# Output stages of a two-layer encoder step: gate rows requested ahead of the residual, weights split in place

## The reference

```
for layer in 0, 1:
    h = rms_norm(x, norm_g[layer]) * (1 + scale) + shift      # scale, shift, gate from the conditioning
    z = h @ w_in                                              # layer 0: 8 groups of 512 columns, and 2 index groups
    ...                                                       # attention of the layer, 16 heads of 64 columns
    mixed = attention_out * silu(gates_from_z)                # gates_nat in DRAM
    y = mixed @ w_out                                         # 1024 x 1024
    x = x + gate[:, None] * y
x = rms_norm(x, final_norm_g)
```

## Time and profile before

| | us |
|---|---|
| median of 3 runs | 2069.78 |
| the three runs | 2056.97, 2069.78, 2070.72 |
| the profiled execution's own time | 2069.88 |
| its span | 2068.1 |

### The profile page before, as it was taken

The page is one execution under the profiler, slowest core; times in us unless marked ns, Lnnn a source line. Parts: engine busy times, 40 slices in busy tenths (PEclk is TensorE's granted clock), DMA queues, the critical chain, the costliest instruction groups (busy, mean ns, idle before and its releaser), DMA issues. The chain is left out here.

```text
span 2068.1 us, 34383 instructions
## 1 busy us (share of the span) xinstructions
PE 1728.9 (84%) x12754; PEld 1335.7 (65%) x12754; DVE 1305.5 (63%) x2848; ACT 943.7 (46%) x1885; POOL 240.5 (12%) x337
## 2 busy tenths in 40 slices
PE   5693488999998985899996895979996999998697
PEld 2460256888876863677774674858774776776476
DVE  2632464787999953778886443661556777777554
ACT  4311252224611273668883213528654667776211
POOL 5000100000000102111100000000004222220000
PEclk8795686999999996999998997989997999999899
DMA  7465602442224318977754343342425111110532
GB/s 277 156 192 147 109 9 73 101 128 87 77 66 112 97 46 203 231 211 203 205 134 153 135 160 131 94 108 71 104 62 115 27 39 30 33 26 9 193 97 97
DMA packets 237102, 235.18 MB, mean 114 GB/s; under 512 B 148181, under 2 KB 172021, under 8 KB 234890
## 3 DMA queue, kind: packets, MB, share of 16 engines
q1 hardware_dynamic: 226170, 198.91, 35.5%
q0 software_dynamic: 10768, 34.08, 4.3%
HBM read 173.98 MB, written 58.95 MB: 113 GB/s over the span
## 5 line engine op out<-in xcount | busy, mean ns | idle before, releaser
L351 PE MATMUL PS<-ab_wh,hT 128*128 128x512 f32 x576 | 229.1, 398 | 10.4 <-DVE ab_wl L676 9.8
L353 PE MATMUL PS<-ab_wh,hT 128*128 128x512 f32 x576 | 225.4, 391 | 0.0
L352 PE MATMUL PS<-ab_wl,hT 128*128 128x512 f32 x576 | 225.0, 391 | 0.0
L1125 DVE TENSOR_SCALAR_CACHE_REDUCE topk_junk<-scores,topk_small 128x528 bf16<-128x528 f32 (+6 forms) x224 | 194.6, 916 | 1.3
L2205 DVE CUSTOM_DVE_ANT_0 la_S<-PS,la_mask 128x128 f32<-128x128 f32 (+3 forms) x144 | 107.6, 747 | 41.7 <-PE PS L353 28.5
L351 PE MATMUL PS<-out_wh,out_mT 128*128 128x512 f32 x288 | 121.9, 423 | 10.1 <-DVE out_wl L1693 9.7
L351 PEld LDWEIGHTS PS<-ab_wh,hT 128*128 128x128 f32 x576 | 108.7, 189 | 33.4 <-ACT ab_wh L604 6.7
L1471 ACT ACTIVATE at_P<-at_S,at_nm 128x128 f32<-128x128 f32 (+2 forms) x144 | 110.4, 767 | 31.3 <-DVE at_nm L1516 31.1
L353 PEld LDWEIGHTS PS<-ab_wh,hT 128*128 128x128 f32 x576 | 108.5, 188 | 23.3
L352 PEld LDWEIGHTS PS<-ab_wl,hT 128*128 128x128 f32 x576 | 108.9, 189 | 21.5
L352 PE MATMUL PS<-out_wl,out_mT 128*128 128x512 f32 x288 | 118.4, 411 | 0.0
(11 more groups left out here) (415 smaller groups left out, 4597.6 us busy)
## 6 DMA issues: line engine op xcount, KB each, us to landing
ab_w<-in_ab_w_in SPq DMA_DIRECT2D x64, 256.0 KB, 2.9
out_g<-scratch_gates_nat SPq DMA_DIRECT2D x18, 512.0 KB, 5.9
mod_ada_w<-in_ada_w SPq DMA_DIRECT2D x8, 1024.0 KB, 13.0
mod_w<-in_ada_w SPq DMA_DIRECT2D x16, 512.0 KB, 4.9
mod_w<-in_ada_w SPq DMA_DIRECT2D x8, 1024.0 KB, 5.8
at_kc<-in_cache_a_k SPq DMA_DIRECT2D x8, 1024.0 KB, 9.5
at_vc<-in_cache_a_v SPq DMA_DIRECT2D x8, 1024.0 KB, 8.0
at_kc<-in_cache_b_k SPq DMA_DIRECT2D x8, 1024.0 KB, 7.6
```

The costliest lines, as they stand in the source:

```text
L351: nc.tensor.matmul(out, x[0], w[0], start=start, stop=False)
L352: nc.tensor.matmul(out, x[0], w[1], start=False, stop=False)
L353: return nc.tensor.matmul(out, x[1], w[0], start=False, stop=stop)
L1125: go(V.tensor_scalar(mark, x, limit, 0.0, op, ALU.add, accum_out=cnt[:, m:m + 1]), 0 if m == M - 1 else 1)
```

## The change

- `mixed_out`: SP requests gate rows two tiles ahead: `load_x(i)`, then `load_gates(i + 2)`. The DVE has a written order: splits of weights between the first gate steps and low halves; then per tile y, the low half of tile i+2, the norm, and `gate_rows(i + 3)`. The last tile's y, square, scale and store go in two halves of 512 columns. TensorE turns tile 1 between the sixth and seventh k-tile of tile 0, and walks both column halves of tile 0 k by k.
- All weights have their own place: the raw tile and its low half share memory (`overlaid`), so `wl = raw - wh` is written over `raw`, and there is no ring. In `projection` all k-tiles of group g+1 are requested at step (g, 1), once the group before in that slot is multiplied, and split in steps 2 to 8.
- `OutLoads`: two k-tiles and the first gate rows of the output stage are requested inside the attention, in memory that the attention has done with (`decay`, `stage`, `qr_in` now lie there).
- `Front`: the first group's eight k-tiles of layer 1's projection and its norm rows are requested in stage 1 (behind x 2), and split there by ACT and DVE, two per tile in tiles 2 to 5. The block that loaded the norm rows is gone.
- `scores` lies at the other side of SBUF.

Core of the diff:

```diff
+def overlaid(nc, stack, name, shape, side="left"):
+    with nc.sbuf_tensor(f"{name}_raw", shape, F32, side=side) as raw:
+        pass
+    return raw, stack.enter_context(nc.sbuf_tensor(name, shape, F32R, side=side))
...
+    def fetch_weights(self, sp):                      # Front
+        c = self.c
+        sp.dma_start(c.latent_g[:, 0:QL], dram(c.i["c_q_norm_g"], 0, [[0, P], [1, QL]])).then_inc(self.g_in, 16)
+        sp.dma_start(c.latent_g[:, QL:], dram(c.i["c_kv_norm_g"], 0, [[0, P], [1, KVL]])).then_inc(self.g_in, 16)
+        for k in range(KT):
+            sp.dma_start(self.raw[:, k, :], c.i["c_w_in"][0, k * P:(k + 1) * P, 0:QL + KVL]).then_inc(self.w_in[k], 16)
+    def split_high(self, act, k):
+        act.wait_ge(self.w_in[k], 16)
+        self.nc.scalar.activation(self.wh[:, k, :], self.raw[:, k, :], ACT.Copy).then_inc(self.w_hi, 1)
+    def split_low(self, dve, k):
+        dve.wait_ge(self.w_hi, k + 1)
+        self.nc.vector.tensor_tensor(self.wl[:, k, :], self.raw[:, k, :], self.wh[:, k, :], ALU.subtract).then_inc(self.w_lo, 1)
...
-        split_steps.setdefault((g - 1, k * NT // groups[g].kt), []).append(k)
+            split_steps.setdefault((g - 1, 2 + k * (NT - 2) // groups[g].kt), []).append(k)
...
-            if r >= RING:
-                sp.wait_ge(w_lo, r - RING + 1)
+            if g:
+                sp.wait_ge(w_lo, first[g])
+            if before_in_slot(g) is not None:
+                sp.wait_ge(mm_done, NT * (before_in_slot(g) + 1))
+            for k in range(groups[g].kt):
+                for at, frm, m in parts:
+                    sp.dma_start(raw[slot(g)][:, k, at:at + m], groups[g].w[k * P:(k + 1) * P, frm:frm + m]).then_inc(w_in[k], 16)
...
+                if s < len(steps) and steps[s][1] == 1:
+                    load_weights(sp, steps[s][0] + 1)
...
+            sp.wait_ge(maxed, head_at(H - 1, QT - 1) + 1)     # end of branches_ab's SP list
+            out.fetch_weights(sp)
+            sp.wait_ge(built, 6)
+            out.fetch_gates(sp)
...
+            for k in range(2, KT):                            # mixed_out, SP
+                sp.dma_start(raw(k), out.w_dram[k * P:(k + 1) * P, :]).then_inc(w_in[k], 16)
+                if k == 3:
+                    load_gates(1)
+            load_x(0)
             sp.dma_start(gate[:], ...).then_inc(rows_in, 16)
-            sp.wait_ge(w_lo, KT)
+            sp.dma_start(sample_gate[:], ...).then_inc(rows_in, 16)
...
+            load_gates(2)
+            load_x(1)
+            load_gates(3)
             for i in range(2, NT):
-                rows(i)
+                load_x(i)
+                load_gates(i + 2)
+                if front and i == 2:
+                    front.fetch_weights(sp)
...
+            chain(nc.vector.reciprocal(rinv[:], c.sums[:]))   # mixed_out, DVE
+            gate_rows(0)
+            for k in range(2):
+                split_low(k)
+            low(0)
+            for k in range(2, 4):
+                split_low(k)
+            gate_rows(1)
+            for k in range(4, KT):
+                split_low(k)
+            low(1)
+            gate_rows(2)
+            dve.wait_ge(rows_in, 32 + 16 * last_layer)
+            for i in range(NT - 1):
+                dve.wait_ge(mm_done, i + 1)
+                dve.wait_ge(x_in[i % 2], 16 * (i // 2 + 1))
+                ...                                           # y = PS * gate + x
+                if i + 2 < NT:
+                    low(i + 2)
+                dve.wait_ge(std_done, i + 1)
+                ...                                           # reciprocal, scale
+                if i + 3 < QT:
+                    gate_rows(i + 3)
+                if front and 2 <= i < 6:
+                    for k in range(2 * i - 4, 2 * i - 2):
+                        front.split_low(dve, k)
...
+            turn(0)                                           # mixed_out, TensorE
+            pe.wait_ge(mT_lo, 1)
+            for k in range(KT):
+                pe.wait_ge(w_lo, k + 1)
+                for a in range(2):
+                    last = multiply(0, a, k)
+                if k == 5:
+                    turn(1)
+            last.then_inc(mm_done, 1)
+            for i in range(1, NT):
+                if i + 1 < NT:
+                    turn(i + 1)
+                pe.wait_ge(mT_lo, i + 1)
+                if i >= 2:
+                    pe.wait_ge(y_read, i - 1)
+                for a in range(2):
+                    for k in range(KT):
+                        last = multiply(i, a, k)
+                    if a == 0 and i == NT - 1:
+                        last.then_inc(half_done, 1)
+                last.then_inc(mm_done, 1)
```

More of the change, by code:

```diff
@@ L63 @@
 STORE_NAMES = [f"{p}_nat_out{n}" for p in ("ix", "ab", "c") for n in range(4)] + ["cum_out"] + [
-    f"out{l}_{m}{n}" for l in range(2) for n in range(2) for m in ("stored", "row")]
+    f"out{l}_{m}{n}" for l in range(2) for n in range(2) for m in ("stored", "row")] + ["out0_w_in0", "out0_w_in1", "out0_g_in0"]
 def store_semaphore(name):
@@ L598, in split_high @@
             def split_high(g, k):
[L599 to L605, removed]
+                act.wait_ge(w_in[k], w_loaded(g, k))
+                nc.scalar.activation(wh[slot(g)][:, k, 0:groups[g].n], raw[slot(g)][:, k, 0:groups[g].n], ACT.Copy).then_inc(w_hi, 1)
+            for k in range(0 if front else groups[0].kt):
                 split_high(0, k)
-                if front and k % 4 == 3:
-                    front.act(act, k // 4)
+            for i in range(2 if front else 0):
+                front.act(act, i)
             for s in range(len(steps) + LAG):
@@ L675, in split_low @@
                 n = groups[g].n
-                nc.vector.tensor_tensor(wl[slot(g)][:, k, 0:n], wt[:, (first[g] + k) % RING, 0:n], wh[slot(g)][:, k, 0:n], ALU.subtract).then_inc(w_lo, 1)
-            for k in range(groups[0].kt):
+                nc.vector.tensor_tensor(wl[slot(g)][:, k, 0:n], raw[slot(g)][:, k, 0:n], wh[slot(g)][:, k, 0:n], ALU.subtract).then_inc(w_lo, 1)
+            for k in range(0 if front else groups[0].kt):
                 split_low(0, k)
-                if front and k % 4 == 3:
-                    front.dve(dve, k // 4)
+            if front:
+                dve.wait_ge(front.g_in, 32)
+            for i in range(2 if front else 0):
+                front.dve(dve, i)
             for s in range(len(steps) + LAG):
@@ new lines, in _ @@
+            dve.wait_ge(std_done, NT)
+            chain(nc.vector.reciprocal(total, total))
+            for a in range(2):
+                if last_layer:
+                    nc.vector.scalar_tensor_tensor(out=yt[:, HALVES[a]], in0=yt[:, HALVES[a]], scalar=total, in1=fg[:, HALVES[a]],
+                                                   op0=ALU.mult, op1=ALU.mult).then_inc(y_done, 1)
+                else:
+                    nc.vector.tensor_scalar(x[:, i % 2, HALVES[a]], yt[:, HALVES[a]], total, None, ALU.mult).then_inc(row_done, 1)
```

341 lines of the change are left out of this document (175 added, 166 removed).

## The result

The kernel after takes 2006.98 us (median of 4 runs, 2002.08 to 2010.29), the kernel before 2063.38 us (median of 4, 2054.06 to 2070.72), run beside it. The ratio is 0.973, with a 95% interval from 0.967 to 0.978: 56 us less, where the forecast was 2001 against 2070, 69 us less. The profiled execution of after took 2010.29 us with a span of 2008.6 us; that of before 2069.88 with 2068.1. So 59.5 us of span went. The same kernel run again beside the last experiment had a median of 2008.38 us and a ratio of 0.973 (0.970 to 0.976).

The account below looks back on a forecast made before the run. Output-stage tiles (stage 1 layer 0, stage 2 layer 1) were taken as bound by the gates' DMA latency plus TensorE, and by slow stage starts. Terms summed to -69.2 us from 2069.88, giving 2000.7, predicted as 2001; range 1988 to 2024.

Parts of the forecast that it names:

- Steady tiles: Output stages: earlier gate requests leave TensorE as the bound, 11.77 us per tile against 15.32 and 14.14 us.
- Start of the stages: Output stages: steady part begins 24 us after the DVE's first instruction; each stage lasts 118 us, saving 31.5 and 27.8.
- The DMA rate: Output-stage weight loads: 410 GB/s from the trace kept over the skill's 358, which would make the gain some 4 us smaller.
- Prefetch in the attention: First two weight tiles and gate rows arrive during SP's idle wait at no cost; without that cover, up to 4 us later.
- From stage 1 to the second projection: Between layer 0's output stage and the next projection: stage end 1.5, block 5.0, earlier projection start 4.9 us saved.
- The eighth split: Large projection: the later last weight split makes TensorE wait entering group 6; net cost 5.2 us, bounds 0 and 9.
- Rings: Start of two projections: loading weights without the ring removes waits, 1.5 us each, 3.0 us saved in all.
- Group changes of the second projection: Second projection: two changes of group cost 0.5 us each, 1.0 us in all.
- A: Output stages: gates asked for earlier but tiles do not close up, 42 us of gain lost, 2043 us; 5%.
- B: Stage starts: repeated rows delay tile 2's gates by 6 us per stage and the clock falls again, 2015 us; 15%.
- C: Three projections: later splits and the weight burst stall TensorE at all 16 group changes, slower, 2108 us; 3%.
- D: Projections: DVE or ACT hide the split's delay altogether and the second projection starts sooner, 1994 us; 17%.

Follow-up runs that it names:

- the last experiment: Kernel after with tile 1 turned behind weight 2, tile 2's gate rows ahead of x 0, sample's gate rows requested later, splits ending in step 6: 1997.97 us, ratio 0.968.
- experiment 2: Kernel before with one edit: in the output stages' steady part, gate rows of tile i+1 requested ahead of x of tile i: 2030.34 us, ratio 0.983.
- experiment 7: Kernel after with the steady part's gate rows requested one x later, behind the x of the tile before and its wait: 2025.79 us.
- experiment 8: Kernel after with tile 1 of an output stage turned behind weight 2, not weight 5, and nothing else: 1998.75 us.
- experiment 4: Kernel after with the second projection's first weights and norm rows requested at the end of stage 1 and split at the projection's start: 2013.73 us.
- experiment 1: Kernel after with the splits of the next group's weights ending in step 7, not step 8: median 2005.3 us, ratio 0.971.
- experiment 3: Kernel after with the first two weight tiles and first gate rows requested at each output stage's start, not inside the attention: 2015.61 us.
- Version 5: Kernel after with splits ending in step 7, tile 1 turned behind weight 2, tile 2's gate rows requested ahead of x 0: 1996.16 us, ratio 0.968.

## Why the prediction was right, and where its sum was 10 us off

**Steady tiles: right.** The distances are 11.78 us where the sum had 11.77. Experiments 2 and 7 show that the request's place alone does it, with and without the rest of the change.

**Start of the stages: right in time, with a wait that it did not name.** 24 us to the steady part was predicted, 24.5 measured, and tile 2's gates landed 17.3 us after their request at 1111.74, 22.2 us after the start (19 to 23 predicted). The splits end 17.0 us after the start (1123.9), where the prediction had 17.8. What it put behind them up to 24 us holds 3.91 us of waiting, which it did not name: tile 1 is turned only behind the sixth weight. Two delays of the same length lay side by side, which experiment 8 shows by taking one away. How little room there is shows in the profiles with the new code and the gate rows of tile 2 where after requests them. In nine stages (after, again after, experiments 4 and 8, stage 1 of 7) TensorE sat idle 1.7 to 2.4 us before tile 2's transposes and its clock stayed at full; in five (experiments 1 and 3, stage 2 of 7) it was 3.1 to 3.6 us, and the granted clock between the first two y was 0.88 to 0.89. Versions 5 and 10 have neither delay, and with 115.0 to 116.1 us they come to the prediction's lower bound of 115.5.

**The DMA rate: the trace decides.** The sum used 410 GB/s for weight tiles. In the line of DMA throughput over 1106.9 to 1131.4 of after (40 slices) the weights run at 395 to 428 for sixteen slices; from the repeated rows on most slices have 154 to 214, the plain rows queued behind them among these:

```profile
GB/s 0 107 127 415 421 395 395 421 408 415 421 415 428 415 395 421 401 421 415 388 334 227 361 174 187 161 187 154 187 167 167 201 167 348 207 214 207 201 94 13
```

The Trainium skill (DMA: Bandwidth & Descriptors, section Bandwidth) puts a core's transfers from HBM at about 358 GB/s, and the prediction weighed that figure alone. The same section gives it as the share of each core when both cores of the HBM domain stream, and 425 GB/s for 16 MB with one core; here one core runs, and the trace agrees with the latter. The 4 us of gain that 358 GB/s would have cost did not go missing: stages 1 and 2 took 118.2 and 118.1 us.

**Prefetch in the attention: right up to the first y.** Priced at nothing with the cover and up to 4 us per stage without; measured 4.2 and 3.5 to the first y, 5.9 and 4.9 by the whole stages (experiment 3).

**From stage 1 to the second projection: right.** 11.4 us forecast and measured. The part that is the early split was 4.9 in the forecast and 4.1 in experiment 4. The other 7.3 go to the block and the last tile's halves, which were not tried apart.

**The eighth split: the mechanism right, the term too small.** 5.2 us forecast (bounds 0 and 9), 9.1 measured. One part is a slip of the sum: the prediction's own numbers, TensorE 7.0 us later and 0.8 us less behind it, give 6.2 and not 5.2. The other is that I let the wait appear entering group 6 alone. Measured against before, TensorE in after is 2.6 us late at its first product, 3.2 at the last of group 4, 12.7 at the last product of group 5's second tile, 5.5 at the end of group 5, 12.6 at the last product of group 6's second tile, 12.2 at the end of group 6 and 12.5 at the end. So entering group 5 costs 9.5 us, of which 7.2 come back inside the group: in before the DVE's backlog holds its tiles at 5.9 to 8.1 us, in after they take 5.9 behind the wait. Entering group 6 costs 7.2 us, near the forecast 7.0, and only 0.4 of it come back. Each of the two prices holds some 1 us and more of half clock, since behind the waits of 7.13 and 6.72 us products take 0.43 us from start to start and not 0.23. Net it is 2.3 us for group 5, 6.7 for group 6 and 0.9 for the groups before and behind, where smaller waits of 1.33 and 0.97 us stand (entering 4 and 7): 9.9 us. ACT and the DVE end 5.0 us behind TensorE and not 5.9, as the prediction had it, which leaves 9.1.

**Rings: wrong.** I gave 3.0 us; nothing came. The wait before the large projection's first product is 6.34 us (6.35 in before), and the small projection's first product starts at 73.80 (73.42). The DVE's eighth split does end 1.6 us sooner after the first product, but from its first product to the next tile's TensorE takes 7.7 us in both, so the splits were not what it waited for. The step that failed is the one that took ACT's 11.0 us of waits for TensorE's: 8.6 us of them are the first transfer, which after has too.

**Group changes of the second projection:** 1.0 us forecast, 2.4 measured (279.9 to 282.4 us from first to last product; the other kernels with the new code had 281.5 to 282.6, the two with the old 279.1 and 280.0).

**What no term of mine covers** is -4.3 us in the attention, +2.7 from the second projection's last product to stage 2, and +2.2 before the large projection once the small projection's start is taken off: 0.6 us in sum, and that they cancel is luck. The -4.3 is the draw of this profile: the second one of after has 332.2 us there, 5.4 more than before. From the large projection's end to stage 1 the nine profiles with the new code took 322.5 to 332.6 us (mean 328.9), the three with the old 321.7 to 327.2 (325.2); from the second projection's last product to stage 2 the nine took 354.2 to 356.9 and the three 352.4 to 354.2. The change requests rows at the end of both attentions and lays some of their buffers elsewhere, and the prediction put that at nothing. The means differ by 3.7 and 1.8 us, which speaks for a small loss, but no experiment tries it. Experiment 3 leaves the fetch out and has 329.6 and 356.2 us, so the fetch alone is not its cause.

So of the 9.7 us by which the sum missed the measured span, the terms that I mis-sized hold 3.0 (rings), 3.9 (eighth split) and 1.4 (group changes); the rest is this 0.6 and 0.8 in steps of 0.4 and less and in rounding. That the median of 2007 lies only 6 us from the 2001 is in part chance as well: before came to 2063.38 beside it and not to 2069.78, so that the difference, 56 us, is 13 us short of the forecast 69.

Of the rivals, A is refuted by experiment 2 (and its price counted seven tiles per stage where five wait). B's 2015 did not come, since tile 2's gates ended a wait of at most 0.2 us in after; but its clock did fall again in experiments 1 and 3, at 1.6 to 1.8 us per stage. C is refuted by the size of the waits: two changes of group in sixteen cost over 6 us. D, that the later split is hidden altogether, is refuted by the 9.1 us.

## What to carry to other kernels

Look in the queue of an engine that only waits and issues for a request that stands behind a wait it does not need; here moving one request in SP's order gave 34 of the 59 us of the two stages. When a producer's last piece moves behind a consumer's last tile in the producer's program order, the price is that tile's whole chain on the producer, at each change where the producer is behind (7.13 and 6.72 us here). The consumer wins it back only where the producer's backlog held it up anyway, and one step earlier in the order costs nothing. A wait that disappears when its releaser is moved may leave another of the same length beside it, so take both away before you judge either.

## What the runs showed of the hardware that was not expected

TensorE's clock in a stretch before the large projection decides 14 us of the whole time. After 3.7 us of idle it runs the sample's index scores, in before and in experiment 2 with the same instructions, as that edit lies in the output stages. In before, the clock stays at the lower level (1.2 GHz, granted 0.52) for the whole 34 us, in experiment 2 it returns to full (0.82 on average) and the large projection begins 14.1 us sooner (324.40 against 338.47). The window of before, then that of experiment 2:

```profile
290.00:324.00 34.00, 32.37 (x95) 21.85 (x96) 6.95 (x11) 9.38 (x17) 0.00 (x0) 0.52 0.00 0
```

```profile
290.00:324.00 34.00, 26.59 (x112) 18.25 (x112) 8.29 (x13) 11.40 (x20) 0.00 (x0) 0.82 0.08 26
```

Of twelve profiles seven had the first kind (0.50 to 0.56), five the second (0.75 to 0.85), with old and new code in both. What decides between them in a given run stays open; both had TensorE at 0.95 in the 40 us before. The spread of the runs of one kernel (2052 to 2072 us for before, beside the first four experiments) is about of this size.
